# Four conditioning units of the second mixer: between the turns of its heads, or inside the first four steps of its attention

## The reference, cut to what matters

```
# first block, layer 1 (the second mixer): latent attention with 8 heads
a = h @ w_a; cq, ckv, k_pe = split(a)
q = (rms_norm(cq, q_a_gain) @ w_qb).reshape(b, s, 8, 192)
kv = (rms_norm(ckv, kv_a_gain) @ w_kvb).reshape(b, s, 8, 256)
q, k = rms_norm(q), rms_norm(k); rope on the last 64 of 192
x = x + causal_attention(q, k, v) @ w_out
x = x + hier_moe(rms_norm(x), ...)            # 64 experts

# second block: six rows of 1024 that depend on c only
mod = silu(c) @ w_ada + b_ada                 # (1024) @ (1024 x 6144)
sh1, sc1, ga1, sh2, sc2, ga2 = split(mod, 6)
```

## Time and profile before

| | |
|---|---|
| median of three runs | 1505.35 us (1504.63 to 1506.43) |
| span of the profiled execution | 1503.6 us |
| TensorE busy in the profiled execution | 1305.5 us (87%) |
| VectorE, ScalarE, GpSimd busy | 666.2, 273.6, 131.2 us |
| mean rate of all DMA | 342 GB/s |
| turns of the latent heads, by the trace | from 649.06 us of the span |
| its attention, first scores | 660.49 us |
| experts of the second mixture, first products | 726.92 us |

### The profile page before, as it was taken

The page is one execution under the profiler, slowest core; times in us unless marked ns, Lnnn a source line. Parts: engine busy times, 40 slices in busy tenths (PEclk is TensorE's granted clock), DMA queues, the critical chain, the costliest instruction groups (busy, mean ns, idle before and its releaser), DMA issues.

```text
span 1503.6 us, 25645 instructions
## 1 busy us (share of the span) xinstructions
PE 1305.5 (87%) x9730; PEld 809.0 (54%) x9730; DVE 666.2 (44%) x1622; ACT 273.6 (18%) x756; POOL 131.2 (9%) x201
## 2 busy tenths in 40 slices
PE   9999999866776679999999766776678999999997
PEld 4455565433443343666665433443344874899943
DVE  3874534221222123672534221222122635699976
ACT  2153211100010011372211100010001134222200
POOL 1312000000000000211000000000000143222100
PEclk9999999898898889999999988898899999999999
DMA  8978799999999999959899999999999991654400
GB/s 286 404 285 341 291 420 404 421 421 421 422 422 422 422 422 396 368 204 420 321 421 401 420 421 422 422 422 422 422 422 400 380 364 41 210 169 169 168 28 29
DMA packets 120555, 513.63 MB, mean 342 GB/s; under 512 B 12296, under 2 KB 46796, under 8 KB 69144
## 3 DMA queue, kind: packets, MB, share of 16 engines
q1 hardware_dynamic: 118576, 507.30, 84.5%
q0 software_dynamic: 1728, 5.12, 0.9%
q10 hardware_dynamic: 168, 0.09, 0.0%
HBM read 511.39 MB, written 1.08 MB: 341 GB/s over the span
## 4 chain that ended last, share of the span: by engine, by line
PE 56%; DMA 20%; SPq 18%; issue 3%; DVE 2%; ACT 1%; ACTq 0%; POOL 0%; POOLq 0%; DVEq 0%
SPq L1872 14%; DMA ring<-in_moe_w_up 13%; PE bank L1415 8%; PE bank L2689 8%; PE bank L575 8%; DMA BC<-in_moe_w_up 5%; PE bank L2724 4%; PE bank L1430 3%; PE bank L1401 3%; PE bank L453 3%; PE bank L2314 3%; PE bank L465 3%; SPq L1881 3%; PE bank L1443 2%; SPq L1899 2%
## 5 line engine op out<-in xcount | busy, mean ns | idle before, releaser
L1415 PE MATMUL bank<-ring,hT 128*32 128x256 f32 (+1 forms) x2848 | 281.9, 454 | 131.2 <-DMA ring<-in_moe_w_up 67.1
L1415 PEld LDWEIGHTS bank<-ring,hT 128*32 128x32 f32 (+1 forms) x2848 | 149.4, 131 | 232.6 <-issue 169.6
L1707 DVE TENSOR_SCALAR pT<-pT 128x256 f32<-128x256 f32 x34 | 10.0, 294 | 406.9 <-ACT pT L1839 406.9
L1415 PE MATMUL bank<-BC,hT 128*32 128x256 f32 (+1 forms) x1120 | 148.5, 435 | 42.4 <-DMA ring<-in_moe_w_up 22.6
L1401 PEld LDWEIGHTS bank<-gtab,hn 128*128 128x128 f32 x1088 | 129.3, 192 | 15.4 <-issue 14.3
L1401 PE MATMUL bank<-gtab,hn 128*128 128x128 f32 x1088 | 132.6, 275 | 0.1
L1415 PEld LDWEIGHTS bank<-BC,hT 128*32 128x32 f32 (+1 forms) x1120 | 76.1, 127 | 80.6 <-issue 64.0
L1430 PE MATMUL bank<-ring,gtab 128*32 128x512 f32 (+1 forms) x768 | 116.8, 596 | 2.5 <-DMA ring<-in_moe_w_down 2.5
L1443 PE MATMUL bank<-hT,A 128*128 128x512 f32 x256 | 118.3, 605 | 0.0
L575 PE MATMUL bank<-ring,hT 128*128 128x512 f32 (+3 forms) x288 | 99.9, 505 | 0.8 <-DMA ring<-in_diff_w_in 0.5
L1839 ACT ACTIVATE pT<-bank 128x256 f32<-128x256 f32 x34 | 13.0, 383 | 460.1 <-PE bank L1415 460.1
(11 more groups left out here) (390 smaller groups left out, 1943.6 us busy)
## 6 DMA issues: line engine op xcount, KB each, us to landing
ring<-in_moe_w_gate SPq DMA_DIRECT2D x90, 1024.0 KB, 24.8
ring<-in_moe_w_up SPq DMA_DIRECT2D x88, 1024.0 KB, 25.5
ring<-in_moe_w_down SPq DMA_DIRECT2D x88, 1024.0 KB, 26.3
BC<-in_moe_w_gate SPq DMA_DIRECT2D x38, 1024.0 KB, 24.6
BC<-in_moe_w_up SPq DMA_DIRECT2D x32, 1024.0 KB, 25.0
BC<-in_moe_w_down SPq DMA_DIRECT2D x28, 1024.0 KB, 26.3
ring<-in_w_ada SPq DMA_DIRECT2D x24, 1024.0 KB, 13.9
ring<-in_w_up SPq DMA_DIRECT2D x22, 1024.0 KB, 7.4
```

The source lines that it names most:

```text
L1415: i = nc.tensor.matmul(GATE[q * cap:(q + 1) * cap, part * FF:(part + 1) * FF], xg[:, c, q * cap:(q + 1) * cap], u[:, c, :], start=(c == 0) ...
```

## The change

The four multiplications of `cond2` leave the turn stage, which now runs its 16 fills in one piece. A new object, `conditioning_left`, is given to the latent attention as `beside`: it puts one unit in each of the first four steps (items 0 to 3), between the scores of item i+3 and the sum of item i. ScalarE copies the bank to `modrow` behind the exponential of item 6, in step 4. The store of the row goes to GpSimd's queue, with a semaphore of its own.

```diff
@@ class Conditioning
+            def copy(self, act):
+                act.wait_ge(*done_with(self.units[-1]))
+                if self.earlier:
+                    self.earlier.ready(act)
+                nc.scalar.activation(modrow[:, :], self.bank[:, :], ACT.Copy).then_inc(self.copied.sem, 1)
+
+            def store(self, eng):
+                eng.wait_ge(*self.copied(1))
+                eng.dma_start(mod_dram[self.g * UNIT:(self.g + 1) * UNIT].rearrange("(q n) -> q n", q=4),
+                              modrow[0:P:32, :]).then_inc(self.stored.sem, 16)
@@
         def latents_tensor(pe):
-            t4.tensor(pe, 0, 4)
+            t4.tensor(pe)
             pe.wait_ge(*pkv.copied(8))
-            cond2.tensor(pe, 4, 6)
-            t4.tensor(pe, 4, 6)
-            cond2.tensor(pe, 6, 8)
-            t4.tensor(pe, 6)
@@
+        class ConditioningLeft:
+            def keys_ready(self, pe, i):
+                pass
+            def tensor(self, pe, k):
+                if 1 <= k <= DC - cond2.spread + 1:
+                    cond2.tensor(pe, cond2.spread + k - 2, cond2.spread + k - 1)
+                if k == HEADS + 1:
+                    cond2.bank_read(pe)
+            def scalar(self, act, i):
+                if i == DC - cond2.spread + 1:
+                    cond2.copy(act)
+            def vector(self, dve, i):
+                pass
@@
-                             head_turned=latent_head_turned, last_turned=last_keys_turned)
+                             head_turned=latent_head_turned, last_turned=last_keys_turned, beside=conditioning_left)
@@ gpsimd
             heads_gpsimd(pool)
+            cond2.store(pool)
             m2.gpsimd(pool)
@@ scalar
-            t4.scalar(act, 0, 6)
-            cond2.scalar(act)
-            t4.scalar(act, 6)
+            t4.scalar(act)
```

More of the change, by code:

```diff
@@ L1090, in build, with __init__ @@
         class Conditioning:
-            def __init__(self, g, at_bank, spread=DC):
+            def __init__(self, g, at_bank, spread=DC, earlier=None):
                 self.g, self.bank, self.units, self.spread = g, bank[at_bank], [], spread
-                self.copied, self.stored = shared("mod_copied", 1), shared("mod_stored", 16)
+                self.copied, self.stored = shared("mod_copied", 1), shared("mod_stored" if earlier is None or g == 2 else "mod_stored_by_pool", 16)
+                self.earlier = earlier
                 self.formed, self.n = shared("sum_formed", spread), 0
@@ L1133, in tensor @@
                     i.then_inc(unit_done.sem, 1)
-            def scalar(self, act):
[L1136 to L1142, removed]
+            def copy(self, act):
[7 more added lines that the diff above has]
+                              modrow[0:P:32, :]).then_inc(self.stored.sem, 16)
+            def scalar(self, act):
+                self.copy(act)
+                self.store(act)
             def bank_read(self, eng):
@@ L1148, in ready @@
                 eng.wait_ge(*self.stored(16))
-        cond1, cond2, cond3 = Conditioning(0, 3), Conditioning(1, 3, 5), Conditioning(2, 3)
+        cond1 = Conditioning(0, 3)
+        cond2 = Conditioning(1, 3, 5, cond1)
+        cond3 = Conditioning(2, 3, DC, cond2)
         cond1.plan(DC)
@@ L2166, in latent_head_turned @@
                 t4.left(pe, K6)
-            if i == HEADS - 1:
-                cond2.bank_read(pe)
+        class ConditioningLeft:
[11 more added lines that the diff above has]
+                pass
+        conditioning_left = ConditioningLeft()
         def last_keys_turned(dve, k):
```

## The result

Thirteen runs of each kernel: the changed one takes 1508.86 us (median, 1507.59 to 1509.88), the one before 1505.65 us (1504.63 to 1506.63). The ratio is 1.0022, with a 95% interval of 1.0015 to 1.0029, so 3.2 us are lost. The forecast was 1507.8 us, 2.5 us over before.

The account below looks back on a forecast made before the run. The prediction took the edited stretch to be bound by engines, not weights. Turns -0.63, step 0 +0.63, three further steps +2.31 and ScalarE's copy +0.2 gave +2.5 us: 1507.8 us, with 8 in 10 held by 1505.3 to 1509.7.

Parts of the forecast that it names:

- within 0.2%: Whole kernel: outcome that the time differs from before by no more than 0.2%, 3.0 us; chance 0.64.
- What leaves the turns: Turn stage: 3.7 us of TensorE's time leave, but VectorE's copies limit the gain to 0.63 us.
- the sum: All terms added: +2.5 us, 1507.8 us; as an outcome +1.7 to +3.2 us, chance 0.6.
- The steps: First attention steps: 1.87 us each with a unit, 2.31 us more over three; step 0 adds 0.63 us.
- My upper bound: Attention steps: with 0.12 us more at each entry into the 32-column mode, 0.5 us more (2.8).
- A unit's length: Units on TensorE: 1.00 us for one alone between scores, 0.93 us in a pair.
- ScalarE and step 5: Attention: the row's copy takes ScalarE 0.60 us, 0.35 hidden by TensorE's scores, 0.2 us show.
- The store, SyncE's queue: Store on GpSimd has 40 us of cover and costs nothing; last unit ends before loads need its ring slots.
- The weights behind: Loads up to 820 us wait for engines 2.5 us late, so the weights' stream moves as one with the work.
- The units are hidden: Rival, attention: idle time in each step hides the units, leaving 1501.6 to 1504.7 us; chance 0.07.
- The weights absorb the delay: Rival, behind the attention: delay only shortens a later DMA wait, time stays at 1505 to 1506 us; chance 0.13.
- Each unit empties the array twice: Rival, attention: passes into and out of the 32-column mode cost 0.36 us more a step; +3.9 us, 1509.2 us; chance 0.2.

Follow-up runs that it names:

- e3: Changed kernel with the multiplications of units 5, 6 and 7 of the second group taking 32 columns in place of 512; 1505.02 us, one timed run.
- e5: Changed kernel with all four units in step 0 of the attention, in place of one in each of four steps; 1508.83 us, one timed run.
- e2: Changed kernel with the units back between the turns; row's copy stays in step 4, its store on GpSimd's queue; 1505.62 us, ratio to before 0.9999.
- e1: Against the kernel before, only the row's store moved, to GpSimd's queue; units and row's copy between the turns; 1505.47 us, ratio 1.0001.
- e7: Changed kernel with each of the four units multiplied twice in its step; 1511.62 us, one timed run.
- e6: Changed kernel with the units in pairs, 4 and 5 in step 0, 6 and 7 in step 2; 1509.07 us, one timed run.

## Why the prediction came out as it did

**Right in sign, place and mechanism; short by 0.5 us in the traces and 0.7 in the medians.** The time of 1508.86 us lies in the range of 1505.3 to 1509.7. Of the three outcomes I gave "within 0.2%" the highest chance; the measured 0.22% lies just over that bound, with an interval that spans it.

- *What leaves the turns*: -0.63 forecast, -0.61 measured. That 3.7 us of TensorE's time leave and only 0.6 us are gained is shown by the waiting that took the units' place: the two idle times, 2.44 us together, and the 1.1 us inside the second row. That VectorE's copy of fill 6 holds fill 10 is shown by the 0.97 us; fills 10 to 15 then take 2.68 us, as the 2.69 of the sum.
- *The steps*: this is the term that was mis-sized. I took 1.87 us a step, measured is 1.97; three steps give 2.61 us in place of 2.31. In step 0 I took +0.63 us and measured +0.81, of which 0.11 are the entry and the other 0.07 stand in the scores ahead of it (0.61 us to the unit, 0.54 in the next steps), for a reason I did not look for. Together 0.48 us too little. The step that failed is the price of an entry: "an entry costs about 0.07 us, and the sum has it already". The 1.00 us of the earlier trace rows holds the way out of the mode; the way in, 0.11 us, stands ahead of the unit. My upper bound named it ("0.12 us more at each entry") from the gap behind the eight transposes, and I took it for a wait for a bank; e3 (the gap is there whatever the unit's length) and e5 (no such gap between units in a row) show that it goes with the entry.
- *A unit's length*: 0.93 in a pair was 0.86 of streaming and half of one way out. So the two figures of the prediction, read rightly, gave 2 x (1.00 - 0.93) = 0.14 us for the way out, and not 0.07 for a whole entry. For a lone unit it made no difference, since 1.00 was taken from a lone one.
- *ScalarE and step 5*: 0.2 forecast, 0.13 by e2 against e1, and 0.15 by the changed kernel, where items 3 to 6 take 23.83 - 20.15 = 3.68 us against 3.53 before.
- *The store, SyncE's queue*: nothing forecast, nothing found. e1 and e2 have the store on GpSimd and are not slower than before. By the rule of the Trainium skill, "SBUF — State Buffer", Who interferes with whom, VectorE could have been held there, and no run here shows it: in the changed kernel VectorE's store of a sum that falls into the issue, at 673.04 us, takes 0.35 us as the others do.
- *The weights behind*: forecast to move as one with the work, and they do up to the first long wait: it comes 2.97 us later and is as long as before.

**The rivals.** "The units are hidden" falls by the 1.97 us steps. "The weights absorb the delay" falls by the wait of 24.16 us, as long as before; e7 leaves room for a small part. "Each unit empties the array twice" fits in kind and not in size: 0.25 us in and out was measured, of which the sum lacked 0.11 a step; the rival had put in 0.36 more and 3.9 us in all. The loss of 3.2 us in the medians lies halfway between the sum's 2.5 and that 3.9. The rule of the Trainium skill, "TensorEngine Tiling (Array Packing)", Key Properties, is that a change of tiling mode drains TensorE. The traces agree with it, 0.11 us in and 0.14 out, about the same where the unit is 32 columns long, but they do not show the drain itself.

**What stays open.** Traces give 2.97 us to the first wait for weights, medians 3.2. The difference is within the uncertainty of the medians. In the two profiled executions it arises behind that wait: from the first transpose to the end of the span they differ by 857.79 - 854.54 = 3.25 us. But single executions scatter there: e5 and e6 end 857.18 and 858.15 us behind the first transpose, 1 us apart, although their items 3 are 0.11 us apart. Whether e1 is truly 0.4 us faster than before, as its trace says, no timed run can tell.

## What to carry to other kernels

Work that is moved off one engine's busy stretch gains only what the next engine in line lets go, and costs its whole length where the same engine is full: ask for the room at the new place (here 0.23 us a step for 1.1 us of work), not whether other engines wait there. When two edits come together, price them apart: here, by the traces, the small one (a store taken from a queue that copies wait behind) held most of the gain, and the large one nearly all of the loss. Small foreign work put between others should be priced from start of the work before it to start of the work behind it, in and out.

## What the hardware showed that was not expected

Four multiplications into the four 32-column parts take 0.86 us in a row and 1.11 us alone between products of the full array: 0.11 us on the way in, 0.14 on the way out. The way in was the same for 512 and for 32 columns. Weight loads, which are taken ahead by 0.22 us between full-array products and by 0.42 us within the mode, began only with their product at either border. A store issued by ScalarE behind its own copy held ScalarE for 1.72 us from the start of the copy, of which 1.01 us are the issue; the same store from GpSimd took 0.67 us of a queue that had nothing else to do.
